# Five norms of a two-block transformer kernel: first block scaled from SBUF, a gate sum and the modulation sums moved, the middle norm's last tile in halves

## The chip, the cores and the metric

The kernel runs on one core of one Trainium2 chip. The metric is the device time of one execution in microseconds (us), as the median of the runs.

## The reference, cut to what matters

Two transformer blocks run over x, 256 tokens of width 1024, in fp32. The norms are what the change is about:

```python
def rmsnorm_2(x, w):
    xf = x.astype(jnp.float32)
    y = xf * lax.rsqrt(jnp.mean(xf * xf, axis=-1, keepdims=True) + EPS)
    return (y * w.astype(jnp.float32)).astype(x.dtype)
...
# first block
u = rmsnorm(h, norm_mix_g[layer])          # norm 0
p = jnp.einsum('bsd,de->bse', u, w_in[layer]) + b_in[layer]
...
u = rmsnorm(h, norm_ffn_g[layer])          # norm 1
z = silu(u @ w_ffn_gate) * (u @ w_ffn_up); h = h + z @ w_ffn_down
return rmsnorm(h, norm_final_g)
# second block
mod = (c_act @ w_ada[l] + b_ada[l])[:, None, :]
sh_m, sc_m, g_m, sh_f, sc_f, g_f = jnp.split(mod, 6, axis=-1)
h = rmsnorm_2(x, norm_mix_w[l]) * (1 + sc_m) + sh_m        # norm 2, on top of norm_final_g's
...
x = x + g_m * (concat(y_ssd, y_att) @ w_out[l])
h = rmsnorm_2(x, norm_ffn_w[l]) * (1 + sc_f) + sh_f        # norm 3
x = x + g_f * conv_ffn(h, w_up[l], ffn_conv_w[l], w_down[l])
return rmsnorm_2(x, final_norm_w)                          # norm 4
```

Norm 2 does two norms in one: the first block's last (with the gain `norm_final_g`) and the second block's first. It therefore needs the sum of squares of the residual and of `Y`, the residual times that gain.

## The kernel before, in words

**The weights** stream from HBM in panels of 4 blocks of 128 rows by 512 columns (1 MB each), two panels ahead, through four slots `raw`. Each product is made of three: ScalarE rounds a panel to `wH` (line 680, 1.9 us), VectorE subtracts to get the rest `wL` (line 1049 by `split_lo`, 2.3 us), and TensorE multiplies high with high, high with low, low with high (lines 1616 and 1619). The normalised activations are split in the same way, into `p1H` and `p1L`. A panel of the "cm" kind is 4 tiles by 4 row blocks by 3 products = 48 products of 256 columns.

**The order of the work** is a list written by hand, `timeline()` (line 119), that every engine walks in order; each engine does its part of each entry and waits on semaphores for the others. So a wait on one engine holds everything behind it there.

**A norm** (lines 748, 1105, 1679, one for each engine) stands between the last panel of one product and the first of the next: norm 0 before `q0`, norm 1 between `out1` and `f0`, norm 2 between `down1` and `xs`, norm 3 between `oo1` and `u0`. Its steps are: VectorE adds the last tile to the residual `res`; ScalarE squares it with a sum (`square`, line 704) and takes the root (`root`, line 726); VectorE inverts it (`turn_over`, line 1087); TensorE spreads the inverse roots over all partitions into `rb`, half of PSUM bank 7 (line 1701); ScalarE copies `rb` to SBUF as `rbs` (line 769). Meanwhile TensorE transposes the residual's 8 column blocks into PSUM (`turn`, line 1556); block 7 lands where block 1 was, so its two transposes are made only after part 0 of the next product (`last_turn`, line 1572). For each block k, VectorE then writes `TMP[k]` = block times gain times `rbs` (line 1137), ScalarE rounds it to `p1H[k]` (lines 781 and 783), VectorE subtracts to `p1L[k]` (`low`, line 1123), and TensorE starts on block k of part 0 of the next product. The loop over k on VectorE is: `TMP[k]`, then `low(k-1)`, then pieces of a weight panel's low half (`first_lo`, `later_lo`). ScalarE has the high halves in the same places, and behind the last `p1H` it goes to the `split_hi` of the next product's next panel, in norm 2 behind one more root, `Ra`, that needs VectorE's sum at line 1151.

**The gates.** In norms 1 and 3, TensorE also sums two gate vectors over the partitions (`gate_sum`, line 1577), the second one ahead of the spread; ScalarE copies out the first, VectorE the second (line 1115).

**The modulation** of the second block is accumulated panel by panel on VectorE and summed over the partitions by TensorE (`ada_sum`, line 1583), 4 products of 64 columns for 512 values, and read by VectorE (`read_ada`, line 1096). Five such sums stand in the feed-forward part (`f3`, `f5`, `f7`, `f9`, `down0`), three inside norm 2 ahead of its spread.

**The last tile in halves.** In norms 1, 3 and 4 the last tile is computed as two halves of 256 columns, the second in bank 6, so that the first can be added and squared while TensorE is on the second (`last_tile`, line 1159). In norm 2 it was one tile of 512 columns.

Of the kernel before, what the change touches and what calls it, by code (L numbers as in the profile page):

```python
# [101 lines left out]
HALF = {1: 1, 3: 2, 4: 3}  # L102
# [16 lines left out]
def timeline():  # L119
# [56 lines left out]
    gemm("down0", [], [("ada_sum", "down0")])  # L176
# [19 lines left out]
def build(nc, IN, out):  # L196
# [17 lines left out]
    with ExitStack() as ctx:  # L214
# [56 lines left out]
        on.in_brow = ctx.enter_context(nc.semaphore("in_brow"))  # L271
        on.half_done = ctx.enter_context(nc.semaphore("half_done"))
# [183 lines left out]
        XA, pre2 = sb("XA", [P, 1]), sb("pre2", [P, 1])  # L456
# [20 lines left out]
        def adaps(where, x):  # L477
            b, c = (x // 2, x % 2 * 4 * NSUM) if where == "norm" else (7, 0)
            return ps[:, b, c:c + 4 * NSUM]

# [9 lines left out]
        HALVES = {"out1": EV["bh1", 2], "oo1": (on.pt_done, 9), "dd1": EV["u9", 2]}  # L490
# [172 lines left out]
        def _(act):  # L663
# [40 lines left out]
            def square(n, i, j):  # L704
# [6 lines left out]
                if n != 2 and 2 * i + j == 3:  # L711
                    act.wait_ge(on.res_half, HALF[n])
                    nc.scalar.activation(sqj[:, 0:T], res[:, 1, W:W + T], ACT.Square, accum_out=XA[:]).then_inc(on.sq_half, 1)
                    cs = slice(W + T, D)
                    if n == 4:
                        store(1, 0)
                act.wait_ge(*EV[f"{RES[n]}{i}", j])
                nc.scalar.activation(sqj[:, cs.start % W:W], res[:, j, cs], ACT.Square,
                                     accum_out=XS[:, i, j:j + 1]).then_inc(on.sq_done, 1)
                if n == 2:  # L720
                    act.wait_ge(on.y_done, 2 * i + j + 1)
                    act.wait_ge(on.sq_done, squares(n, 2 * i + j + 1))
                    nc.scalar.activation(sqj, Y[:, j, half(i)], ACT.Square,
                                         accum_out=YS[:, i, j:j + 1]).then_inc(on.ysq_done, 1)
# [23 lines left out]
            def norm(n):  # L748

                table(ACT.Sqrt)  # L750
                for j in range(TB):
                    if n:
                        square(n, 1, j)
                    else:
                        square_x(j)
                    if n != 2:
                        root(n, j)
                if n == 4:
                    return
                if n == 2:  # L760
                    for j in range(TB):
                        root(n, j)
                if n == 0:
                    first_hi(0, 0, 1)
                if n in GATE_OF:
                    act.wait_ge(on.gate_psum, 2 * GATE_OF[n] + 1)
                    nc.scalar.activation(GATE[GATE_OF[n]][0], ps[:, 2 * GATE_OF[n], :], ACT.Copy).then_inc(on.gate_done, 1)
                act.wait_ge(on.rb_psum, n + 1)
                nc.scalar.activation(rbs, rb, ACT.Copy).then_inc(on.rb_copy, 1)
                for k in range(KD):  # L770
# [4 lines left out]
                    elif n and 0 < k <= KP:  # L775
                        later_hi(n, k - 1)
# [260 lines left out]
        def _(dve):  # L1037
# [48 lines left out]

            def turn_over(n, j):

                if n == 2:
                    dve.wait_ge(on.ysq_done, 3 + j)  # L1090
                    stt(S2[:, j:j + 1], XS[:, 1, j:j + 1], EPS, YS[:, 1, j:j + 1], ALU.mult,
                        ALU.add).then_inc(on.s2_done, 1)
# [12 lines left out]
            def norm(n):  # L1105
                if n in (0, 2):
                    turn_over(n, 0)
                if n == 4:
                    scaled(0, 0)
# [3 lines left out]
                if n in GATE_OF:  # L1113
                    dve.wait_ge(on.gate_psum, 2 * GATE_OF[n] + 2)
                    v.tensor_copy(GATE[GATE_OF[n]][1], ps[:, 2 * GATE_OF[n] + 1, :]).then_inc(on.gate_done, 1)
                if n == 2:
                    read_ada("norm")
                    dve.wait_ge(on.ada_done, 8)
                    stt(am[:], mod[:, 8:16], 1.0, pc("norm_mix_w_2", 0, 8), ALU.add, ALU.mult).then_inc(on.mod_done, 1)
                    stt(af[:], mod[:, 32:40], 1.0, pc("norm_ffn_w_2", 0, 8), ALU.add, ALU.mult).then_inc(on.mod_done, 1)  # L1120
                    dve.wait_ge(on.mod_done, 1)
# [37 lines left out]
            def last_tile(name, n):  # L1159
# [4 lines left out]
                if n == 1:  # L1164
                    tt(left, o[:, 0:T], left, ALU.add).then_inc(on.res_half, 1)
                    step(tt(right, o[:, T:W], right, ALU.add))
                    turn_over(n, 0)
                    dve.wait_ge(on.tile_done, TILE[name, 1])
                    tt(right, o2, right, ALU.add).then_inc(on.evac_dve, 1)
                else:  # L1170
# [7 lines left out]
                    dve.wait_ge(on.res_half, HALF[n])  # L1178
# [3 lines left out]
                dve.wait_ge(on.sq_half, HALF[n])  # L1182
# [754 lines left out]
```

## Time and profile before

| | us |
|---|---|
| runs before: median (lowest to highest) of 3 | 819.65 (819.58 to 819.81) |
| the profiled execution's own time | 819.11 |
| its span, first to last instruction | 817.4 |
| TensorE busy | 796.6 (97%) |
| VectorE busy | 592.8 (73%) |
| ScalarE busy | 495.1 (61%) |

TensorE's granted clock is full in all 40 slices of the page. The profiled execution is 0.54 us below the median, and 1.7 us of it lie outside the span. Busy times of matmuls overlap one another, so the distance from one start to the next is what to read, not the duration in the row.

### The profile page before, as it was taken

The numbers are of one execution on the slowest core, as the hardware profiler recorded it, in microseconds if no ns is written. First come the engines' busy times: TensorE is split into PE (matmuls) and PEld (weight loads), VectorE is DVE, ScalarE is ACT, GpSimd is POOL, SyncE is SP. The second block draws the span as 40 slices with busy tenths as digits, with TensorE's granted clock in tenths as the row PEclk, the third lists the DMA queues.
The fourth block names the chain that finished last, engine by engine and source line by source line (L and its number), as shares of the span: only waits on it lengthen the run. The fifth ranks groups of instructions, "written<-read, shape, count | busy, mean of one in ns | idle before, by whom it ended". The sixth has DMA issues, their size and how long they took to land.

```text
span 817.4 us, 14238 instructions
## 1 busy us (share of the span) xinstructions
PE 796.6 (97%) x5944; PEld 743.7 (91%) x5944; DVE 592.8 (73%) x767; ACT 495.1 (61%) x744; POOL 15.8 (2%) x36
## 2 busy tenths in 40 slices
PE   8999999999999999999999999999999999999996
PEld 8988879999999889999998888899788999999885
DVE  5575685639756868887878886897778977787463
ACT  6777788568836456344444256856756776666452
POOL 3000000000200000000000000000000000000000
PEclk9999999999999999999999999999999999999999
DMA  8873634447553558889898993644351865645611
GB/s 295 287 251 111 206 104 155 155 155 235 164 169 104 171 189 275 274 287 297 263 298 272 342 349 100 235 152 155 102 162 55 275 190 175 199 136 205 229 55 52
DMA packets 105664, 161.15 MB, mean 197 GB/s; under 512 B 4464, under 2 KB 51840, under 8 KB 105600
## 3 DMA queue, kind: packets, MB, share of 16 engines
q1 hardware_dynamic: 105456, 159.97, 59.6%
q8 instruction: 47, 0.77, 0.4%
q10 hardware_dynamic: 144, 0.26, 0.1%
q14 instruction: 17, 0.14, 0.0%
HBM read 159.16 MB, written 1.06 MB: 196 GB/s over the span
## 4 chain that ended last, share of the span: by engine, by line
PE 87%; DVE 7%; ACT 4%; issue 2%; DMA 0%; DVEq 0%; ACTq 0%
PE ps L1616 54%; PE ps L1619 22%; DVE wL L1049 2%; PE ps L1545 2%; ACT wH L680 2%; DVE arena L1049 1%; PE ps L1772 1%; ACT arena L932 1%; DVE arena L1052 1%; PE ps L1590 1%; PE ps L1609 1%; PE ps L1739 1%; PE ps L1819 1%; PE ps L1816 1%; PE ps L1804 0%
## 5 line engine op out<-in xcount | busy, mean ns | idle before, releaser
L1049 DVE TENSOR_TENSOR wL<-raw,wH 128x2048 fp32r<-128x2048 f32 (+2 forms) x133 | 282.9, 2131 | 120.7 <-ACT wH L680 119.5
L1616 PE MATMUL ps<-p1H,wH 128*128 128x256 f32 x1256 | 358.9, 286 | 5.8 <-DVE p1L L1049 1.8
L1616 PE MATMUL ps<-p1L,wH 128*128 128x256 f32 x1256 | 355.3, 283 | 0.0
L1616 PE MATMUL ps<-p1H,wL 128*128 128x256 f32 x1256 | 355.3, 283 | 0.0
L680 ACT ACTIVATE wH<-raw 128x2048 fp32r<-128x2048 f32 (+1 forms) x121 | 225.1, 1867 | 123.7 <-PE ps L1616 65.5
L1616 PEld LDWEIGHTS ps<-p1H,wH 128*128 128x128 f32 x1256 | 240.8, 192 | 9.1 <-issue 6.8
L1616 PEld LDWEIGHTS ps<-p1L,wH 128*128 128x128 f32 x1256 | 240.9, 192 | 0.3 <-issue 0.2
L1616 PEld LDWEIGHTS ps<-p1H,wL 128*128 128x128 f32 x1256 | 240.9, 192 | 0.0
L1619 PE MATMUL ps<-wH,zH 128*128 128x512 f32 x172 | 67.0, 390 | 0.0
L1619 PE MATMUL ps<-wH,zL 128*128 128x512 f32 x172 | 66.9, 389 | 0.0
L1619 PE MATMUL ps<-wL,zH 128*128 128x512 f32 x172 | 66.9, 389 | 0.0
L1052 DVE SCALAR_TENSOR_TENSOR arena<-arena,par 128x256 f32<-128x256 f32 x124 | 50.7, 479 | 9.4 <-ACT arena L864 6.9
L798 ACT ACTIVATE arena<-ps 128x256 f32<-128x256 f32 x86 | 30.1, 378 | 26.2 <-PE ps L1616 25.8
L1052 DVE SCALAR_TENSOR_TENSOR arena<-raw,cact,arena 128x512 f32<-128x512 f32 x56 | 42.0, 751 | 1.7
L1049 DVE TENSOR_TENSOR arena<-arena 128x512 f32<-128x512 f32 (+3 forms) x41 | 35.1, 871 | 6.6 <-ACT arena L819 2.6
L1619 PEld LDWEIGHTS ps<-wH,zH 128*128 128x128 f32 x172 | 32.3, 188 | 6.7
L1619 PEld LDWEIGHTS ps<-wH,zL 128*128 128x128 f32 x172 | 32.3, 188 | 6.7
L1619 PEld LDWEIGHTS ps<-wL,zH 128*128 128x128 f32 x172 | 32.3, 188 | 6.6
L1616 PE MATMUL ps<-pyH,wH 128*128 128x256 f32 x128 | 36.6, 286 | 0.0
L1616 PE MATMUL ps<-pyL,wH 128*128 128x256 f32 x128 | 36.2, 283 | 0.0
L1616 PE MATMUL ps<-pyH,wL 128*128 128x256 f32 x128 | 36.2, 283 | 0.0
L1619 PE MATMUL ps<-wH,p1H 128*128 128x512 f32 (+1 forms) x92 | 34.4, 374 | 0.0
(274 smaller groups left out, 956.9 us busy)
## 6 DMA issues: line engine op xcount, KB each, us to landing
raw<-in_w_in SPq DMA_DIRECT2D x38, 1024.0 KB, 5.2
raw<-in_w_ada SPq DMA_DIRECT2D x24, 1024.0 KB, 5.2
raw<-in_w_up SPq DMA_DIRECT2D x44, 512.0 KB, 4.9
raw<-in_w_ffn_gate SPq DMA_DIRECT2D x22, 512.0 KB, 4.7
raw<-in_w_ffn_up SPq DMA_DIRECT2D x22, 512.0 KB, 6.3
raw<-in_w_ffn_down SPq DMA_DIRECT2D x10, 1024.0 KB, 5.4
raw<-in_w_down SPq DMA_DIRECT2D x10, 1024.0 KB, 5.2
raw<-in_w_out SPq DMA_DIRECT2D x8, 1024.0 KB, 5.0
```

Source lines behind the costliest of these rows:

```text
L680: nc.scalar.activation(wH[:, q % NHL, 0:nk, 0:wd], raw[:, i % NRAW, 0:nk, 0:wd], ACT.Copy).then_inc(on.w_hi, 1)
L798: nc.scalar.activation(dst(m), ps[:, t[1], 0:T], f, **bias).then_inc(on.evac_act, 1)
L932: ins = nc.scalar.activation(p, s if kind == 1 else p, ACT.Exp, scale=scale, bias=NM[:, u % 2, h:h + 1], accum_out=SU[:, u % 2, h:h + 1])
L1049: return v.tensor_tensor(o, a, b, op)
L1052: return v.scalar_tensor_tensor(out=o, in0=a, scalar=s, in1=b, op0=op0, op1=op1)
L1545: return nc.tensor.transpose(o, i, ident[:])
L1590: last = mm(adaps(where, x)[:, t * NSUM:(t + 1) * NSUM], ACC[a + x][:, t * P:(t + 1) * P], ones[:, 0:NSUM], start=True, stop=True)
L1609: last = mm(ps[:, bank, 0:T], at_[:, k0 + k, P:2 * P], wt[:, slot, k, half_of * T:half_of * T + T], start=st and x == 0, stop=k == nk - 1 ...
L1616: last = mm(ps[:, t[1], 0:T], wt[:, slot, k, t[2]:t[2] + P], at_[:, k0 + k, :], start=st, stop=en)
L1619: last = mm(ps[:, t[1], 0:t[3]], at_[:, k0 + k, t[4] * P:(t[4] + 1) * P], wt[:, slot, k, t[2]:t[2] + t[3]], start=st, stop=en)
L1739: last = mm(o, aQ[r, h // 2, n * P:(n + 1) * P], kk[r, ks], start=False, stop=a == nh - 2)
L1772: last = mm(ps[C * x:C * x + C, PVB[u], pair * P:(pair + 1) * P], vv, PT[u][:, slot(nh, hh) * nk + kb, :], start=kb == 0, stop=kb == nk - 1)
```

## The change

1. ScalarE copies transposed block 0 to SBUF (`TMP[:, 0]`), and VectorE scales block 0 from that copy with `rb` in PSUM. The copy of `rb` to `rbs` comes after `p1H[0]` on ScalarE, and `low(0)` comes ahead of `TMP[1]` on VectorE.
2. The transposes of block 6 move from inside the norm to `last_turn`, behind part 0 of the next product.
3. The second gate sum stands behind the spread, in bank 3, and is copied out by ScalarE.
4. The modulation sums: none at `down0` any more, two in norm 2 ahead of the spread, two in norm 2 behind the copy of `rb`; each product has 32 columns instead of 64. `am` is computed at `f9`, `af` behind the last `low` of norm 2. The columns of `w_ada` are loaded in another order.
5. Norm 2's last tile is computed in halves.
6. Norm 0 has four filler products behind its transposes instead of two.

```diff
-ADA_COL = (4, 5, 6, 7, 8, 9, 0, 1, 2, 3, 10, 11)
+ADA_COL = (4, 5, 0, 1, 2, 3, 6, 7, 8, 9, 10, 11)
-SUM_AT = {"f3": (2, 1), "f5": (3, 1), "f7": (4, 1), "f9": (5, 1), "down0": (6, 1), "norm": (7, 3)}
+SUM_AT = {"f3": (2, 1), "f5": (3, 1), "f7": (4, 1), "f9": (5, 1), "norm": (6, 2), "post": (8, 2)}
-NSUM = 64
+NSUM = 32
-HALF = {1: 1, 3: 2, 4: 3}
+HALF = {1: 1, 2: 2, 3: 3, 4: 4}
+PART = {1: 1, 2: 2, 3: 4, 4: 5}
-    gemm("down0", [], [("ada_sum", "down0")])
+    gemm("down0")
-        HALVES = {"out1": EV["bh1", 2], "oo1": (on.pt_done, 9), "dd1": EV["u9", 2]}
+        HALVES = {"out1": EV["bh1", 2], "down1": (on.tmp_done, 16), "oo1": (on.pt_done, 9), "dd1": EV["u9", 2]}
...
 ScalarE, square(n, i, j)
+                    if n == 2:
+                        act.wait_ge(on.res_half, PART[n] + 1)
+                        nc.scalar.activation(sqj[:, T:W], Y[:, 1, W:W + T], ACT.Square, accum_out=YA[:]).then_inc(on.sq_half, 1)
+                        act.wait_ge(on.sq_half, PART[n] + 1)
...
 ScalarE, norm(n)
-                    if n != 2:
-                        root(n, j)
+                    root(n, j)
-                if n == 2:
-                    for j in range(TB):
-                        root(n, j)
+                act.wait_ge(on.ut_psum, 4 * n + 1)
+                nc.scalar.activation(TMP[:, 0], un(0), ACT.Copy).then_inc(on.un0_copy, 1)
                 if n in GATE_OF:
                     act.wait_ge(on.gate_psum, 2 * GATE_OF[n] + 1)
                     nc.scalar.activation(GATE[GATE_OF[n]][0], ps[:, 2 * GATE_OF[n], :], ACT.Copy).then_inc(on.gate_done, 1)
-                act.wait_ge(on.rb_psum, n + 1)
-                nc.scalar.activation(rbs, rb, ACT.Copy).then_inc(on.rb_copy, 1)
                 for k in range(KD):
...
-                    elif n and 0 < k <= KP:
-                        later_hi(n, k - 1)
+                    elif n and 1 < k <= KP + 1:
+                        later_hi(n, k - 2)
...
+                    if k == 0:
+                        act.wait_ge(on.rb_psum, n + 1)
+                        nc.scalar.activation(rbs, rb, ACT.Copy).then_inc(on.rb_copy, 1)
+                    if k == 0 and n in GATE_OF:
+                        act.wait_ge(on.gate_psum, 2 * GATE_OF[n] + 2)
+                        nc.scalar.activation(GATE[GATE_OF[n]][1], ps[:, 3, :], ACT.Copy).then_inc(on.gate_done, 1)
...
 VectorE, norm(n)
-                if n in GATE_OF:
-                    dve.wait_ge(on.gate_psum, 2 * GATE_OF[n] + 2)
-                    v.tensor_copy(GATE[GATE_OF[n]][1], ps[:, 2 * GATE_OF[n] + 1, :]).then_inc(on.gate_done, 1)
...
-                dve.wait_ge(on.rb_copy, n + 1)
                 for k in range(KD):
                     if k in (4, 6, 7):
-                        dve.wait_ge(on.ut_psum, 3 * n + {4: 1, 6: 2, 7: 3}[k])
-                    stt(TMP[:, k], un(k), gain(n, k), rbs, ALU.mult, ALU.mult).then_inc(on.tmp_done, 1)
-                    if k:
+                        dve.wait_ge(on.ut_psum, 4 * n + {4: 2, 6: 3, 7: 4}[k])
+                    if k == 0:
+                        dve.wait_ge(on.un0_copy, n + 1)
+                        dve.wait_ge(on.rb_psum, n + 1)
+                    if k == 1:
+                        low(0)
+                        dve.wait_ge(on.rb_copy, n + 1)
+                    stt(TMP[:, k], un(k) if k else TMP[:, 0], gain(n, k), rbs if k else rb, ALU.mult,
+                        ALU.mult).then_inc(on.tmp_done, 1)
+                    if k > 1:
                         low(k - 1)
...
                 low(KD - 1)
                 if n == 2:
+                    read_ada("post")
+                    dve.wait_ge(on.ada_done, 8)
+                    stt(af[:], mod[:, 32:40], 1.0, pc("norm_ffn_w_2", 0, 8), ALU.add, ALU.mult).then_inc(on.mod_done, 1)
                     dve.wait_ge(on.sq_done, squares(2, 4))
+                    step(tt(XS[:, 1, 1:2], XS[:, 1, 1:2], XA[:], ALU.add))
                     tt(Ra[:], XS[:, 0, :], XS[:, 1, :], ALU.add).then_inc(on.sum_final, 1)
...
 VectorE, last_tile(name, n)
-                if n == 1:
+                if n < 3:
                     tt(left, o[:, 0:T], left, ALU.add).then_inc(on.res_half, 1)
                     step(tt(right, o[:, T:W], right, ALU.add))
+                    if n == 2:
+                        dve.wait_ge(on.res_half, PART[n])
+                        tt(Y[:, 1, W:W + T], left, gfin[:, W:W + T], ALU.mult).then_inc(on.res_half, 1)
+                        sum2(0)
                     turn_over(n, 0)
                     dve.wait_ge(on.tile_done, TILE[name, 1])
                     tt(right, o2, right, ALU.add).then_inc(on.evac_dve, 1)
+                    if n == 2:
+                        dve.wait_ge(*EV[name, 1])
+                        tt(Y[:, 1, W + T:D], right, gfin[:, W + T:D], ALU.mult).then_inc(on.y_done, 1)
...
 TensorE
             def last_turn(n):
+                pe.wait_ge(on.rb_copy, n + 1)
+                turn(n, (6,), range(TB)).then_inc(on.ut_psum, 1)
                 pe.wait_ge(on.tmp_done, 8 * n + 2)
                 turn(n, (7,), range(TB)).then_inc(on.ut_psum, 1)
...
-                mm(ps[:, 2 * g + i, :], ones[:], ACC[10 * g + i], start=True, stop=True).then_inc(on.gate_psum, 1)
+                mm(ps[:, 3 if i else 2 * g, :], ones[:], ACC[10 * g + i], start=True, stop=True).then_inc(on.gate_psum, 1)
...
-                    if n in GATE_OF:
-                        gate_sum(GATE_OF[n], 1)
+                    last.then_inc(on.ut_psum, 1)
                     if n == 2:
                         ada_sum("norm")
...
                     last.then_inc(on.rb_psum, 1)
+                    if n in GATE_OF:
+                        gate_sum(GATE_OF[n], 1)
                     stream_in(n, 1, 1)
                     turn(n, (4, 5), range(TB)).then_inc(on.ut_psum, 1)
-                    pe.wait_ge(on.rb_copy, n + 1)
-                    turn(n, (6,), range(TB)).then_inc(on.ut_psum, 1)
+                    if n == 2:
+                        pe.wait_ge(on.rb_copy, n + 1)
+                        ada_sum("post")
                     if n == 0:
-                        warm(2)
+                        warm(4)
```

## Rows read from the trace of the kernel before

**Rows 1.** The page, busy time, share and instructions of each engine.

```profile
PE 796.6 (97%) x5944; PEld 743.7 (91%) x5944; DVE 592.8 (73%) x767; ACT 495.1 (61%) x744; POOL 15.8 (2%) x36
```

**Rows 2.** Waits of TensorE: waited for, us in total, times, longest.

```profile
PE ps L1616 <- DVE wL L1049: 0.8, 1, 0.8
```

**Rows 3.** Timeline, TensorE in norm 1: start, us, instruction, idle before.

```profile
296.66 1.04 PE L1545 MATMUL ps<-ident,res 128*128 128x128 f32 x8
297.53 1.02 PE L1581 MATMUL ps<-acc,ones 128*128 128x512 f32 x2
298.39 0.61 PE L1549 MATMUL ps<-ident,R 128*128 128x128 f32 x4
...
301.11 0.35 PE L1616 MATMUL ps<-p1H,wH 128*128 128x256 f32 x1 [1.19 <-DVE p1L L1049]
...
306.93 0.38 PE L1545 MATMUL ps<-ident,res 128*128 128x128 f32 x2
```

**Rows 4.** Timeline, ScalarE in norm 1.

```profile
295.08 0.42 ACT L713 ACTIVATE arena<-res 128x256 f32<-128x256 f32 x1
...
299.04 0.38 ACT L769 ACTIVATE arena<-ps 128x256 f32<-128x256 f32 x1 [1.21 <-PE ps L1549]
...
306.16 1.28 ACT L670 ACT_TABLE_LOAD   x1
...
307.87 0.42 ACT L781 ACTIVATE p1H<-arena 128x256 fp32r<-128x256 f32 x1 [0.21 <-DVE arena L1052]
```

**Rows 5.** Timeline, VectorE in norm 1 and at panel f0.

```profile
299.46 0.88 DVE L1052 SCALAR_TENSOR_TENSOR arena<-ps,par,arena 128x256 f32<-128x256 f32 x2 [0.17 <-ACT arena L769]
...
307.35 0.48 DVE L1052 SCALAR_TENSOR_TENSOR arena<-ps,par,arena 128x256 f32<-128x256 f32 x1 [1.33 <-PE ps L1545]
...
310.13 2.29 DVE L1049 TENSOR_TENSOR wL<-raw,wH 128x2048 fp32r<-128x2048 f32 x1 [0.49 <-ACT wH L680]
```

**Rows 6.** Timeline, VectorE in norm 0 and at panel q0.

```profile
9.45 0.51 DVE L1049 TENSOR_TENSOR p1L<-arena,p1H 128x256 fp32r<-128x256 f32 x1
...
15.82 0.48 DVE L1052 SCALAR_TENSOR_TENSOR arena<-ps,par,arena 128x256 f32<-128x256 f32 x1
...
20.45 2.29 DVE L1049 TENSOR_TENSOR wL<-raw,wH 128x2048 fp32r<-128x2048 f32 x1 [1.38 <-ACT wH L680]
```

**Rows 7.** Timeline, TensorE behind part 0 of q0.

```profile
15.86 0.38 PE L1545 MATMUL ps<-ident,res 128*128 128x128 f32 x2
```

**Rows 8.** Timeline, TensorE in norm 2 and behind product bc.

```profile
498.80 0.36 PE L1616 MATMUL ps<-p1H,wH 128*128 128x256 f32 x1 [1.27 <-issue]
...
525.90 1.06 PE L1545 MATMUL ps<-ident,arena 128*128 128x128 f32 x8 [0.49 <-DVE ADT L1049]
```

**Rows 9.** Timeline, ScalarE in norm 2.

```profile
493.45 0.63 ACT L718 ACTIVATE arena<-res 128x512 f32<-128x512 f32 x1 [1.18 <-DVE res L1049]
...
495.52 0.29 ACT L738 ACTIVATE R<-S,pre 128x1 f32<-128x1 f32 x1 [0.34 <-DVE S L1052]
496.66 0.38 ACT L769 ACTIVATE arena<-ps 128x256 f32<-128x256 f32 x1 [0.85 <-PE ps L1549]
```

**Rows 10.** Timeline, VectorE behind part 0 of xs.

```profile
505.05 0.48 DVE L1052 SCALAR_TENSOR_TENSOR arena<-ps,am,arena 128x256 f32<-128x256 f32 x1 [0.74 <-PE ps L1545]
...
509.70 2.29 DVE L1049 TENSOR_TENSOR wL<-raw,wH 128x2048 fp32r<-128x2048 f32 x1 [2.15 <-ACT wH L680]
```

**Rows 11.** Chain that ended last: start, us, what.

```profile
440.00 0.84 PE ps L1590 x8
...
535.25 1.46 PE ps L1866 x14
```

**Rows 12.** Timeline, TensorE's first product behind norm 3.

```profile
623.29 0.35 PE L1616 MATMUL ps<-p1H,wH 128*128 128x256 f32 x1 [1.37 <-DVE p1L L1052]
```

**Rows 13.** Timeline, VectorE in norm 3 and at panel u0.

```profile
620.27 0.16 DVE L1094 RECIPROCAL R<-R 128x1 f32<-128x1 f32 x1 [0.88 <-ACT R L738]
...
632.39 4.49 DVE L1049 TENSOR_TENSOR wL<-raw,wH 128x2048 fp32r<-128x2048 f32 x2 [0.44 <-ACT wH L680]
```

More of the change, by code:

```diff
@@ L477, in adaps @@
         def adaps(where, x):
-            b, c = (x // 2, x % 2 * 4 * NSUM) if where == "norm" else (7, 0)
+            b, c = (0, x * 4 * NSUM) if where == "norm" else (7, T + x * 4 * NSUM if where == "post" else 0)
             return ps[:, b, c:c + 4 * NSUM]
@@ L710, in square @@
                 cs = half(i)
-                if n != 2 and 2 * i + j == 3:
-                    act.wait_ge(on.res_half, HALF[n])
+                if 2 * i + j == 3:
+                    act.wait_ge(on.res_half, PART[n])
                     nc.scalar.activation(sqj[:, 0:T], res[:, 1, W:W + T], ACT.Square, accum_out=XA[:]).then_inc(on.sq_half, 1)
+                    if n == 2:
+                        act.wait_ge(on.res_half, PART[n] + 1)
+                        nc.scalar.activation(sqj[:, T:W], Y[:, 1, W:W + T], ACT.Square, accum_out=YA[:]).then_inc(on.sq_half, 1)
+                        act.wait_ge(on.sq_half, PART[n] + 1)
                     cs = slice(W + T, D)
@@ L716, in square @@
                         store(1, 0)
+                junk = sqj[:, cs.start % W:W]
                 act.wait_ge(*EV[f"{RES[n]}{i}", j])
-                nc.scalar.activation(sqj[:, cs.start % W:W], res[:, j, cs], ACT.Square,
-                                     accum_out=XS[:, i, j:j + 1]).then_inc(on.sq_done, 1)
+                nc.scalar.activation(junk, res[:, j, cs], ACT.Square, accum_out=XS[:, i, j:j + 1]).then_inc(on.sq_done, 1)
                 if n == 2:
@@ L722, in square @@
                     act.wait_ge(on.sq_done, squares(n, 2 * i + j + 1))
-                    nc.scalar.activation(sqj, Y[:, j, half(i)], ACT.Square,
-                                         accum_out=YS[:, i, j:j + 1]).then_inc(on.ysq_done, 1)
+                    nc.scalar.activation(junk, Y[:, j, cs], ACT.Square, accum_out=YS[:, i, j:j + 1]).then_inc(on.ysq_done, 1)
             def root(n, j):
@@ L1085, in before, with sum2 @@
                     v.tensor_scalar(pre[:], XS[:, 0, :], 1.0 / D, EPS, ALU.mult, ALU.add).then_inc(on.pre_done, 1)
+            def sum2(j):
+                dve.wait_ge(on.ysq_done, 3 + j)
+                stt(S2[:, j:j + 1], XS[:, 1, j:j + 1], EPS, YS[:, 1, j:j + 1], ALU.mult, ALU.add).then_inc(on.s2_done, 1)
             def turn_over(n, j):
[L1089 to L1092, printed above, removed]
                 dve.wait_ge(on.rt_done, 2 * n + j + 1)
@@ L1105, in norm @@
             def norm(n):
-                if n in (0, 2):
+                if n == 0:
                     turn_over(n, 0)
+                if n == 2:
+                    sum2(1)
                 if n == 4:
@@ L1181, in last_tile @@
                     tt(right, gt[:, 0:T], right, ALU.add).then_inc(on.evac_dve, 1)
-                dve.wait_ge(on.sq_half, HALF[n])
-                stt(pre2[:], XA[:], 1.0 / D, pre[:, 1:2], ALU.mult, ALU.add).then_inc(on.pre2_done, 1)
+                dve.wait_ge(on.sq_half, PART[n] + (n == 2))
+                if n == 2:
+                    step(stt(pre2[:], XA[:], EPS, YA[:], ALU.mult, ALU.add))
+                    stt(pre2[:], pre2[:], 1.0 / D, pre[:, 1:2], ALU.mult, ALU.add).then_inc(on.pre2_done, 1)
+                else:
+                    stt(pre2[:], XA[:], 1.0 / D, pre[:, 1:2], ALU.mult, ALU.add).then_inc(on.pre2_done, 1)
                 if n == 4:
@@ L1344, in _ @@
                     read_ada(e[1])
+                    if e[1] == "f9":
+                        dve.wait_ge(on.ada_done, 4)
+                        stt(am[:], mod[:, 8:16], 1.0, pc("norm_mix_w_2", 0, 8), ALU.add, ALU.mult).then_inc(on.mod_done, 1)
                 elif k == "scores":
@@ L1652, in panel @@
                                 pe.wait_ge(*BANKFREE[name, m])
+                            if k == 0 and m == 3 and name in ("f0", "u0"):
+                                pe.wait_ge(on.gate_done, 2 if name == "f0" else 4)
                             last = product(t, k)
@@ L1685, in _ @@
                         stream_in(0, 0, j)
-                        turn(0, range(4), (j,))
+                        last = turn(0, range(4), (j,))
                     if n in GATE_OF:
@@ L1691, in _ @@
                         stream_in(n, 0, 1)
-                        turn(n, range(4), range(TB))
-                    if n in GATE_OF:
-                        gate_sum(GATE_OF[n], 1)
+                        last = turn(n, range(4), range(TB))
+                    last.then_inc(on.ut_psum, 1)
                     if n == 2:
@@ L1831, in _ @@
                     pe.wait_ge(on.u_ready, 24)
+                    pe.wait_ge(on.ada_done, 8)
                     for kk in range(KD):
```

12 lines of the change are left out of this document (5 added, 7 removed).

## The prediction

> **What bounds the kernel now.** I read the page first. TensorE is busy for 796.6 of 817.4 us and VectorE for 73% [rows 1], with the clock full throughout, so a change can gain only the few places where TensorE waits, and can lose wherever it makes a new one. Then I read the waits of TensorE and the timelines of all three engines around the norms. The reader is to see two chains in each norm. The **front chain** is last root, spread, copy of `rb`, `TMP[0]`, `p1H[0]`, `low(0)`, first product: TensorE stands idle at its end, 1.19 us in norm 1 [rows 3], 1.27 in norm 2 [rows 8], 1.37 in norm 3 [rows 12]. The **back chain** starts behind part 0 of the next product: last transposes, `TMP[7]`, `p1H[7]`, then the split of the next product's panel on ScalarE and VectorE. It is nearly late already: behind norm 0 TensorE waits 0.8 us for it [rows 2], and behind norm 1 `wL` is ready at 310.13 + 2.29 = 312.42 [rows 5], while TensorE comes there at 306.93 + 0.14 (two transposes) + 5.8 (48 products at 0.12) = 312.87 [rows 3], 0.45 later. The change works on the front chain and lengthens the back one.
>
> **Norm 1.** Front: the gate sum leaves the path (297.53 to 298.39 [rows 3]) and so does the copy of `rb` (299.04 to `TMP[0]` at 299.46, 0.42 [rows 4, 5]). The spread then starts at about 297.55 and `TMP[0]` at 298.2 instead of 299.46. The new copy of block 0 (0.38, as the copy of `rb` [rows 4]) runs on ScalarE beside the spread, since the transposes end at 297.53; the gate copies stand behind `p1H[0]` or before it is due. `TMP[1]` behind `low(0)` delays block 1 to about 300.9, and it is due at 301.3. So the first product comes 1.2 earlier, at 299.9, and part 0 ends 1.2 earlier, at 305.7.
> Back: the transposes of block 6 are now made only there. Four transposes instead of two cost TensorE 0.22 more (eight take 0.87 [rows 3]). What counts is the order behind them. VectorE reaches `TMP` 0.42 behind the transposes (306.93 to 307.35 [rows 3, 5]): before, that was block 7, now it is block 6, with `low(5)` and block 7 another 0.8 behind (two operations issued 0.4 apart). On ScalarE the table load, 306.16 before and so hidden in the wait for block 7 [rows 4], now stands behind the late `p1H[6]`: 305.7 + 0.42 = 306.15 `TMP[6]`, 306.67 `p1H[6]`, 307.1 table load, 308.5 `p1H[7]` (1.4 behind the load: itself and its small operation), against 307.87 [rows 4]. From `p1H[7]` to the start of `wL` take the 2.26 of before (307.87 to 310.13 [rows 4, 5]): 310.75, ready 313.05. TensorE would come at 305.7 + 0.36 + 5.8 = 311.9 and waits 1.15. Against 312.87 the norm costs **+0.2**. The whole front gain goes into that wait.
>
> **Norm 3.** The gate sum saves nothing: the last inverse root runs from 620.27 to 620.43 [rows 13], when the sum is just done. Left is the copy, 0.42: first product 622.87 instead of 623.29 [rows 12]. Back: there is no table load, but `TMP[7]` is 0.8 later behind part 0, net 0.4 later; `wL` starts 632.76 instead of 632.39 [rows 13] and is ready at 635.05, which is when TensorE came before. **+0.05**.
>
> **Norm 0.** The first product is bound by `low(0)` at 9.45 [rows 6], which does not move. `TMP[1]`, which was made in the wait ahead of it, comes behind it: 0.4 more on VectorE, 0.2 of it reaching block 1. Part 0 ends at 16.06 instead of 15.86 [rows 7]. `TMP[6]` started at 15.82 [rows 6] and now starts at 16.06 + 0.42 = 16.48, 0.66 later, and with it the rest down to `wL` at 20.45 [rows 6], for which TensorE waited already [rows 2]. **+0.66**. The two more filler products run in idle time; the first product comes 0.6 behind their end.
>
> **Norm 2.** The last tile in halves costs TensorE 0.15, hidden by the front chain. For the root, two squares of 512 columns, from 493.45, ended in the root at 495.52 [rows 9]. Now the first root waits for the left half of `Y`, at about 492.8, and four quarter squares follow, 0.42 [rows 4] plus a read, some 0.52 apart, with two waits of 0.1: 493.0 + 2.1 + 0.1 + 0.3 is again 495.5. Bounds: 0.5 earlier, if nothing waits for the first root, to 0.3 later; I take 0. The copy of `rb` leaves the path (0.42 and a little): `TMP[0]` at 496.66 [rows 9] and the first product could start at 498.3 instead of 498.80 [rows 8]. But TensorE's queue now holds, ahead of it, two modulation sums that wait for that copy, and ScalarE makes the copy behind `p1H[0]`: 497.6 to 498.0. A sum takes 0.84 for 8 passes [rows 11], 0.88 with its edges, so the product starts at 498.0 + 1.76 = 499.8, **1.0 later**. Back: `TMP[7]` comes 1.0 + 0.8 later than 505.05 [rows 10]. Behind the last `low` VectorE has four more small operations, two reads, `af` and a sum with its wait, 0.55 together, and ScalarE's root `Ra` and the split stand behind them: `wL` starts 2.35 later than 509.70 [rows 10], at 512.05, and is ready at 514.35, just when TensorE has done its own 1.2 later work (514.5). That is not the end of it. VectorE and ScalarE are a closed chain from there to `ADT`, and TensorE waited 0.49 for that at 525.90 [rows 8]. So product q2 starts the full **+2.35** later.
>
> **The sum at down0** is gone: **-0.88** [rows 11]. The four others of the feed-forward part stay. Narrower products save nothing: passes of 8 columns take 1.46 for 14 [rows 11], 0.104 each, and those of 64 columns 0.84 for 8, 0.105. The order of the columns of `w_ada` moves no byte more or less, and no queue issues another transfer; SyncE's wait for the last `low` of norm 2 passes some 1.8 later, less than TensorE's own delay. `am` at `f9` is 0.1 on an idle engine.
>
> **Sum:** 0.66 + 0.2 + 2.35 + 0.05 - 0.88 = **+2.4 us**. The profiled execution took 819.11, 0.54 below the median; it would take 821.5, and the median 819.65 becomes **822.0**. 0.2%, about what can be told from no change, is 1.6 us: the limits are 818.0 and 821.3.
>
> **Rivals.**
> *A, the back chain does not end anything.* If ScalarE came to each split early enough, 4.2 before TensorE is due, only fronts and transposes would count: norm 0 +0.4, norm 1 -1.0, norm 3 -0.2, norm 2 +1.2, down0 -0.88, together -0.5: **819.2**, not slower. For it: latencies of 0.1 to 0.3 that I carried over may vanish. Against it: the margin before was 0.45 in norm 1 and negative in norm 0, and the transposes of block 6 are moved by the code itself. Chance 0.12.
> *B, narrow products are cheap.* If 32 columns cost half of 64, the four sums at f3 to f9 and the two behind the spread save 0.42 each, 2.5 together: **819.5**. The 8-column rows speak against it. Chance 0.06. The Trainium skill, TensorE: Matmul & The Clock Gate, in its section Step-by-step: what each phase is for, says throughput is purely as many cycles as columns; by that B would hold, and here the trace disagrees.
> *C, it is worse.* The weight transfers behind norm 2 issue late, because SyncE waits for the slots that VectorE frees 2.35 later, and collide: 1 us more, **823.0**. Chance 0.07.
> *D, mixed.* Parts of A in one or two norms, or the roots of norm 2 0.5 earlier: 819.5 to 820.9. Chance 0.15.
> My forecast has 0.60, with 820.9 to 823.0 as its own range.
>
> **Numbers.** The range 819.3 to 823.0 takes in the forecast, D, B and part of A. Slower by over 0.2%: most of the forecast and C, 0.60. Within 0.2%: B, D, A's middle and the forecast's low end, 0.33. Faster: A and B together, or a margin I misread in norm 2, 0.07.
>
> **What would show it.** Right: first product behind norm 1 about 1.2 earlier in the norm, and a new wait of about 1 us for `wL` at f1; in norm 2, 16 passes of sums between the copy of `rb` and the first product, and a wait for `ADT` of 1.5 to 2 instead of 0.49; behind norm 0, 1.4 instead of 0.8 for `wL`. Wrong: no wait for `wL` at f1, passes of the sums under 0.08 apart, or the last root of norm 2 over 0.3 earlier behind the end of down1.

## The result, and the profile of the changed kernel

The changed kernel takes **825.84 us** as the median of four executions (824.78 to 826.78), against 819.73 for the kernel before in the same comparison: a ratio of 1.0073, 95% interval 1.0055 to 1.009. The sign was forecast; the size was not. 822.0 was predicted, and 823.0 was the upper end of the range. The profiled execution took 824.78 with a span of 823.1, so it lies 5.67 above that of the kernel before. It is the fastest of the four; two took 826.6 and 826.8, so the median lies 6.1 above.

The page of the changed kernel, TensorE's busy time and the granted clock in the 40 slices:

```profile
PE 801.0 (97%) x5960; PEld 748.3 (91%) x5960; DVE 592.9 (72%) x771; ACT 497.5 (60%) x754; POOL 16.1 (2%) x36
PEclk9999999999999999999999999999999999999998
```

The page looks like that of the kernel before [rows 1]. Its slices are 20 us wide and a slice of 90% or more shows as 9, so 3 us at a lower clock would not be seen here. Five of TensorE's waits in the changed kernel (us in total, times, longest); two larger entries, 4.4 in seven waits for `arena` and 2.2 at the start, are the same in both kernels:

```profile
PE ps L1572 <- DVE ADT L1056: 1.5, 1, 1.5
PE ps L1645 <- DVE p1L L1056: 1.5, 3, 0.6
PE ps L1645 <- ACT arena L805: 1.4, 2, 0.9
PE ps L1619 <- ACT arena L788: 1.0, 1, 1.0
PE ps L1645 <- DVE wL L1056: 0.9, 1, 0.9
```

Two of these waits were forecast: 1.5 instead of 0.49 for `ADT` (a tensor that VectorE makes and TensorE transposes behind product bc), and 0.9 at f1. That one is put down to ScalarE's copying out of f0's results, with `wL` ready at the same moment, at 314.14. For `wL` in norm 0 1.4 was forecast, and it is 0.9 instead of 0.8. None of them is 3 us long. Where the rest went is seen in the timeline of TensorE in the changed kernel (start, us, instruction, idle before):

```profile
16.45 0.60 PE L1572 MATMUL ps<-ident,res 128*128 128x128 f32 x4
23.85 0.38 PE L1645 MATMUL ps<-p1H,wH 128*128 128x256 f32 x1 [0.89 <-DVE wL L1056]
297.77 1.03 PE L1572 MATMUL ps<-ident,res 128*128 128x128 f32 x8
301.02 0.35 PE L1645 MATMUL ps<-p1H,wH 128*128 128x256 f32 x1 [0.47 <-DVE p1L L1056]
306.84 0.60 PE L1572 MATMUL ps<-ident,res 128*128 128x128 f32 x4
314.20 0.38 PE L1645 MATMUL ps<-p1H,wH 128*128 128x256 f32 x1 [0.89 <-ACT arena L805]
493.93 1.87 PE L1619 MATMUL ps<-ones,arena 128*128 128x32 f32 x16
498.20 1.97 PE L1619 MATMUL ps<-ones,arena 128*128 128x32 f32 x16 [1.03 <-ACT arena L788]
500.01 0.36 PE L1645 MATMUL ps<-p1H,wH 128*128 128x256 f32 x1
...
502.10 0.41 PE L1645 MATMUL ps<-p1H,wH 128*128 128x256 f32 x1
...
503.38 0.41 PE L1645 MATMUL ps<-p1H,wH 128*128 128x256 f32 x1
...
507.33 0.60 PE L1572 MATMUL ps<-ident,arena 128*128 128x128 f32 x4
...
529.93 1.06 PE L1572 MATMUL ps<-ident,arena 128*128 128x128 f32 x8 [1.52 <-DVE ADT L1056]
628.40 0.35 PE L1645 MATMUL ps<-p1H,wH 128*128 128x256 f32 x1 [0.62 <-ACT brow L791]
815.85 0.28 PE L1638 MATMUL ps<-wL,zH 128*128 128x256 f32 x1
```

Five rows of TensorE in the kernel before, which these are measured against:

```profile
6.53 0.60 PE L1545 MATMUL ps<-ident,res 128*128 128x128 f32 x4
...
22.80 0.39 PE L1616 MATMUL ps<-p1H,wH 128*128 128x256 f32 x1 [0.82 <-DVE wL L1049]
...
493.33 2.79 PE L1590 MATMUL ps<-ones,arena 128*128 128x64 f32 x24
...
504.63 0.38 PE L1545 MATMUL ps<-ident,arena 128*128 128x128 f32 x2
...
810.18 0.28 PE L1609 MATMUL ps<-wL,zH 128*128 128x256 f32 x1
```

From 502.10 to 503.38 lie six products, 0.213 each; before, 48 such products and the step to the transposes took 5.82, 0.12 each (301.11 to 306.93 [rows 3]). The granted clock explains it. The changed kernel by stretches (PE, PEld, DVE, ACT and POOL busy, then PEclk, DMA share, GB/s):

```profile
496.00:500.00 4.00, 2.83 (x23) 2.49 (x23) 2.68 (x9) 2.22 (x6) 0.00 (x0) 1.00 0.00 0
500.00:504.00 4.00, 4.00 (x23) 4.00 (x23) 3.63 (x7) 3.01 (x7) 0.00 (x0) 0.59 0.01 4
528.00:531.00 3.00, 1.48 (x12) 1.06 (x10) 0.35 (x2) 2.99 (x3) 0.00 (x0) 1.00 0.90 279
531.00:535.00 4.00, 3.49 (x17) 3.52 (x18) 3.80 (x4) 3.97 (x10) 0.00 (x0) 0.57 0.24 62
```

and the kernel before in the same places:

```profile
500.00:504.00 4.00, 4.00 (x35) 4.00 (x35) 3.88 (x9) 2.42 (x7) 0.00 (x0) 1.00 0.01 4
528.00:532.00 4.00, 4.00 (x36) 4.00 (x35) 4.00 (x7) 3.97 (x6) 0.00 (x0) 1.00 0.30 68
```

Twice, for some 3.4 us each (0.41 of 4 us is missing, at a level of 0.5), TensorE is granted 1.2 GHz instead of 2.4: right behind the thin stretch of norm 2, and right behind the wait for `ADT`. It is counted as fully busy there, with 23 products in 4 us instead of 35. Part 0 of xs takes 7.32 (500.01 to the transposes at 507.33) instead of 5.83 (498.80 [rows 8] to 504.63), so one such stretch costs **1.5**.

With that the time can be laid out by checkpoints. The second column is how much later the changed kernel comes there, the third what was added since the row above, and the fourth how much of that is the lower clock, at 1.5 for each stretch:

| checkpoint | changed | step | of it lower clock | forecast of the step |
|---|---|---|---|---|
| product q1 behind norm 0 (23.85) | +1.05 | +1.05 | | +0.66 |
| transposes of norm 1 (297.77) | +1.11 | +0.06 | | 0 |
| first sum of norm 2 (493.93) | +0.60 | -0.51 | | +0.2 - 0.88 = -0.68 |
| transposes behind `ADT` (529.93) | +4.03 | +3.43 | 1.5 | +2.35 |
| first product behind norm 3 (628.40) | +5.11 | +1.08 | 1.5 | -0.42 |
| last product of dd (815.85) | +5.67 | +0.56 | | +0.47 |

Without the two stretches 2.7 remain, where 2.4 was forecast.

### The profile page after: what moved, and what is told of

Same layout as the page of the kernel before. It is cut to its first block and busy times, and to the rows that moved or that the text cites. A ratio compares the mean times of both kernels' runs of the same rounds, so it can differ in the third digit from the quotient of the medians.

```text
span 823.1 us, 14290 instructions
## 1 busy us (share of the span) xinstructions
PE 801.0 (97%) x5960; PEld 748.3 (91%) x5960; DVE 592.9 (72%) x771; ACT 497.5 (60%) x754; POOL 16.1 (2%) x36
## 3 DMA queue, kind: packets, MB, share of 16 engines
HBM read 159.16 MB, written 1.06 MB: 195 GB/s over the span
```

## The experiments

Twelve kernels ran. The theory behind most of them, **K**: the schedule costs what was forecast, and the rest is a lower granted clock that comes where TensorE stands empty or does thin work. The rival, **L**: the lower clock has another cause, or the schedule itself costs more. Ratios are to the kernel before, measured beside each. The mean clock of an execution is on record for all of them, the place of a stretch only for the one that was profiled.

**Fillers in norm 2** (`warm(4)`: four products of 128 columns on the identity, two passes each, computing nothing that is used), ahead of the wait for the copy of `rb`, where TensorE stood idle for 1.03:

```diff
                     turn(n, (4, 5), range(TB)).then_inc(on.ut_psum, 1)
                     if n == 2:
+                        warm(4)
                         pe.wait_ge(on.rb_copy, n + 1)
```

> The changed kernel with four 128-column filler products in norm 2, between the transposes of blocks 4 and 5 and the wait for the copy of rb, where TensorE stood empty for 1.03 us. In the changed kernel's trace the granted clock is at its lower level (1.2 GHz) for 3.4 us from 500.7 and again for 3.4 us from 531.3. Theory K (the clock): the first stretch follows from that empty stretch with the thin work around it, and costs 1.7 us; with the fillers it is gone, the time is 824.1, the second stretch stays. Rival S (the schedule): the extra time is waits, the clock follows by chance or from the sums' narrow products themselves; the fillers change nothing, 825.8, and the stretch from 500.7 stays.

Measured: 821.72 (821.38 to 823.99), ratio 1.0025 (1.0016 to 1.0034). Rows of this kernel:

```profile
496.63 1.06 PE L1581 MATMUL ps<-ident 128*128 128x128 f32 x8
497.82 1.97 PE L1619 MATMUL ps<-ones,arena 128*128 128x32 f32 x16
...
528.07 1.06 PE L1572 MATMUL ps<-ident,arena 128*128 128x128 f32 x8 [1.51 <-DVE ADT L1056]
...
812.52 0.28 PE L1638 MATMUL ps<-wL,zH 128*128 128x256 f32 x1
```

```profile
500.00:504.00 4.00, 4.00 (x35) 4.00 (x35) 3.29 (x6) 2.64 (x6) 0.00 (x0) 1.00 0.02 4
530.00:534.00 4.00, 4.00 (x36) 4.00 (x35) 4.00 (x7) 3.97 (x7) 0.00 (x0) 1.00 0.24 55
```

Eight passes in a time that was idle anyway make the kernel 4.1 faster than the changed one by the medians, and 3.3 by the profiled executions (821.47 to 824.78). The schedule is the same: from the first sum of norm 2 (493.55 here) to the late sums it is 4.27 in both. From that sum to the transposes behind `ADT` it takes 34.52 instead of 36.00. Both stretches are gone, the second too, against the expectation, though the wait of 1.51 for `ADT` is still there. Why the second went with the first, 30 us behind the fillers, is not shown. The last product comes 2.34 later than before (812.52 to 810.18); the forecast was +2.4.

**Fillers there and ahead of the wait for `ADT`** (six more, in bank 5).

> As the run before, and six more fillers at the transposes behind product bc, where TensorE waited 1.5 us for ADT. Theory K: both stretches at the lower clock are gone, 822.4, which is the time that the prediction gave; its sum of waits was then right and only the clock was left out. Rival S: 825.8. If the second stretch has another cause (the first one's delay), 824.1 and one stretch left.

Measured: 821.64 (821.45 to 822.73), 1.0025 (1.0015 to 1.0035). With the lower clock gone already, more fillers gain nothing.

**The sums as before the change** (64 columns, one at down0, three in norm 2, both factors behind them; everything else changed):

```diff
-SUM_AT = {..., "norm": (6, 2), "post": (8, 2)}
-NSUM = 32
+SUM_AT = {..., "down0": (6, 1), "norm": (7, 3)}
+NSUM = 64
```

> The changed kernel with part 4 undone: one sum at down0 again, three in norm 2 ahead of the spread, none behind it, 64 columns, columns of w_ada in the old order, am and af in norm 2. Theory K: no empty stretch before sums, no lower clock in norm 2; product xs starts 1.5 earlier, q2 2.05 earlier, down0 0.88 later: 825.8 - 3.4 - 2.05 + 0.88 = 821.2, ratio to the kernel before 1.002. Rival S without the clock as a term: 825.8 - 1.2 = 824.6.

Measured: 821.34 (821.06 to 823.39), 1.0025 (1.0016 to 1.0035). Its profiled execution, at 823.39 one of the slower ones:

```profile
500.00:504.00 4.00, 3.54 (x29) 3.57 (x30) 3.73 (x9) 3.33 (x9) 0.00 (x0) 1.00 0.02 4
530.00:534.00 4.00, 3.87 (x20) 3.90 (x21) 4.00 (x5) 3.97 (x8) 0.00 (x0) 0.58 0.19 28
```

Only the second stretch is left, here behind a wait of 1.16 for `ADT`. So it does not need the first. Norm 2 itself holds 24 passes of 64 columns and 1.35 of idle here, and the clock stays up. Of the ten executions three have a mean clock of 0.995 and take 823.0 to 823.4; of the seven at 0.997 or 0.998 six take 821.1 to 821.4. By these clocks the same program gets the stretch in one execution and not in the next.

**Block 6's transposes back in the norm** (in norm 2 behind the two late sums; norm 0 has three filler products instead of four):

```diff
                     turn(n, (4, 5), range(TB)).then_inc(on.ut_psum, 1)
+                    if n == 0:
+                        warm(3)
+                    pe.wait_ge(on.rb_copy, n + 1)
                     if n == 2:
-                        pe.wait_ge(on.rb_copy, n + 1)
                         ada_sum("post")
-                    if n == 0:
-                        warm(4)
+                    turn(n, (6,), range(TB)).then_inc(on.ut_psum, 1)
...
-                pe.wait_ge(on.rb_copy, n + 1)
-                turn(n, (6,), range(TB)).then_inc(on.ut_psum, 1)
                 pe.wait_ge(on.tmp_done, 8 * n + 2)
```

> The changed kernel with part 2 undone: the transposes of block 6 stand in the norm again, behind the copy of rb (in norm 2 behind the two sums as well), so that TMP[6] does not wait for part 0. If the back chain ends what the prediction said: 0.4 gained in norm 0, 0.9 in norm 1 (no wait for wL at f1), 0.4 in norm 3, 0.8 in norm 2 and up to q2, 2.5 together: 823.3, with both stretches at the lower clock still there. If the back chain does not end it, only 0.22 for each of the four norms: 825.0.

Measured: 820.93 (820.11 to 822.35), 1.0017 (1.0007 to 1.0026), 2.4 below what was expected. Five executions lie at 820.1 to 820.4 with a mean clock of 0.996, five at 821.4 to 822.4 with 0.994. The profiled one, of the first kind:

```profile
498.00:502.00 4.00, 4.00 (x23) 4.00 (x23) 3.88 (x8) 3.10 (x7) 0.00 (x0) 0.57 0.02 4
...
530.00:534.00 4.00, 4.00 (x36) 4.00 (x35) 4.00 (x8) 3.98 (x6) 0.00 (x0) 1.00 0.43 119
```

Only the first stretch stands in this trace. The mean clocks fit one stretch in the five faster executions and two in the five slower ones. The wait for `ADT` is down to 1.0. The median of the five slower ones, 822.1, is still 1.2 below what was expected with both stretches; the expectation started from the changed kernel's median, and half of its executions had a lower clock still.

**The same with fillers** (`warm(4)` ahead of the wait in norm 2).

> The kernel with block 6's transposes back in the norm, plus four filler products in norm 2 ahead of the wait for the copy of rb, where TensorE stands idle anyway. The kernel without the fillers took 820.93 with one stretch of lower clock in its faster runs and two in its slower ones, each worth 1.7. Theory K (idle and thin work there bring the lower clock): the stretches go, 818.6 or so, faster than the kernel before. Theory L (the lower clock has another cause): no change from 820.9.

Measured: 818.95 (818.26 to 819.95), 0.9986 (0.9977 to 0.9994), and no stretch of lower clock in its trace before the tail of the kernel. For the stretch in norm 2, K is confirmed a second time.

**Block 6 and the sums both as before**; kept are the copy of block 0, the order of `low(0)`, the late gate sum and the last tile in halves. Norm 0 has three filler products here too.

> The changed kernel with parts 2 and 4 undone: block 6's transposes stand in the norm again, and the sums stand as before the change (64 columns, one at down0, three in norm 2 with both factors behind them). Kept are the copy of block 0, the order of low(0), the second gate sum behind the spread, and the last tile of norm 2 in halves. Schedule theory S (the terms of the prediction hold, and a lower granted clock comes only where TensorE stood nearly empty in norm 2): norm 0 +0.4, norm 1 -1.0, norm 3 -0.2, norm 2 -0.4, so about 818.5, with no stretch of clock at the lower level before the end. Theory K2 (the lower clock comes with the earlier copy of block 0 itself): one such stretch of 3.4 us at the norm or at the wait for ADT, 820.2.

Measured: **818.04** (817.7 to 818.69), 0.9979 (0.997 to 0.9987). This version beats both kernels. Rows of its TensorE, and one of its waits:

```profile
6.99 1.06 PE L1570 MATMUL ps<-ident,res 128*128 128x128 f32 x4
7.84 0.92 PE L1579 MATMUL ps<-ident 128*128 128x128 f32 x4
...
493.40 2.79 PE L1615 MATMUL ps<-ones,arena 128*128 128x64 f32 x24
...
525.77 1.06 PE L1570 MATMUL ps<-ident,arena 128*128 128x128 f32 x8 [0.68 <-DVE ADT L1056]
...
622.76 0.36 PE L1641 MATMUL ps<-p1H,wH 128*128 128x256 f32 x1
```

```profile
PE ps L1641 <- DVE wL L1056: 0.8, 1, 0.8
```

Norm 1 starts at 297.79 here, 1.13 later than before. Most of that comes from norm 0, where four passes take 0.85 (6.99 to 7.84), while before four took 0.44 from 6.53 on; the input itself was there no later (first transposes at 4.37 and 4.42). That is the ratio of the two clock levels, but the windows view gives a granted clock of 1.00 there, so the reason is not shown. Such a slow start differs from one execution to the next. The sums of norm 2 start at 493.40, 0.07 later than before: 1.06 is gained from norm 1 to there. The transposes behind `ADT` come 0.13 earlier, so norm 2 gains 0.20, and the first product behind norm 3 0.53 earlier, which is 0.40 more. These are rival A's terms for norms 1 and 3, about -1.0 and -0.2.

From the executions without lower clock the two withdrawn parts get their prices: block 6 behind the product costs 821.72 - 818.95 = **2.8** (and 821.3 - 818.0 = 3.3 with the old sums), the reordered sums 818.95 - 818.04 = **0.9**. The two kernels of each block 6 pair ran in different comparisons, in which the kernel before took 819.81 and 820.06, so these two prices could be 0.25 larger.

**Norm 0 as before as well** (`rb` copied first, `low(0)` behind `TMP[1]`).

> The kernel with parts 2 and 4 undone, and norm 0 entirely as before the change as well (rb copied first, TMP[0] and TMP[1] from it, low(0) behind them). Theory S: norm 0 gives back its 0.4 to 0.6, so 0.5 below that kernel, about 818.0. Rival: nothing on norm 0's first product or on its wait for wL hangs on the order of these operations, and it takes the same time.

Measured: 818.19 (817.66 to 819.19), 0.9979 (0.9971 to 0.9988): the same time, not 0.5 less. The rival holds, as far as eleven executions of each can tell. The order of these operations in norm 0 is worth nothing that shows.

**Only narrower products, in the kernel before.**

```diff
-NSUM = 64
+NSUM = 32
```

> The kernel before with modulation products of 32 columns instead of 64 and nothing else. Theory S (a pass costs the same at 8, 32 and 64 columns): no difference, 819.7. Rival B (half the columns, half the time): eight sums on the path save 0.42 each, some 3 us, 816.6.

Measured: 819.84 (819.09 to 822.02), 1.0006 (0.9998 to 1.0015). The three sums of norm 2:

```profile
493.31 2.76 PE L1590 MATMUL ps<-ones,arena 128*128 128x32 f32 x24
```

24 passes take 2.76, against 2.79 with 64 columns (493.33 above). Rival B is refuted. But five of its twelve executions take 821.7 to 822.0 at a mean clock of 0.996, where the other seven take 819.1 to 819.9 at 0.998 or 0.999 and none of the 35 executions of the kernel before is under 0.997. So halving the columns seems to bring a stretch of lower clock in some executions. The profiled one had none, so its place isn't shown.

The last four ask what TensorE has to do for the clock to fall. Three of them are the kernel before with one thing added in norm 2.

**Idle only**: the product waits for `low(2)` instead of `low(0)`.

```diff
                     turn(n, (6,), range(TB)).then_inc(on.ut_psum, 1)
+                    if n == 2:
+                        pe.wait_ge(on.u_ready, 19)
```

> The kernel before, in which the first product of xs in norm 2 waits for low(2) instead of low(0). Nothing is computed differently; TensorE only stands idle for some 2.7 us there instead of 1.27. The product comes 1.4 later, and the chain behind it too: without a lower clock 821.1. Theory I (an empty TensorE is enough to bring the lower clock): a stretch of 3.4 us at 1.2 GHz behind it, 1.7 more, 822.8. Theory N (it takes the narrow passes): 821.1, and no such stretch.

Measured: 823.49 (822.35 to 825.33), 1.0043 (1.0031 to 1.0055).

The first product of xs, and the stretch behind it:

```profile
501.63 0.39 PE L1616 MATMUL ps<-p1H,wH 128*128 128x256 f32 x1 [3.06 <-DVE p1L L1052]
```

```profile
502.00:506.00 4.00, 4.00 (x25) 4.00 (x24) 3.28 (x6) 1.91 (x4) 0.00 (x0) 0.62 0.02 4
```

An empty engine, with nothing added to the passes that were there before, is enough: theory I. The Trainium skill, TensorE: Matmul & The Clock Gate, section HAM oscillation: how this bites in real kernels, says that a TensorE left waiting is put back to its lower clock, so that what follows starts slow; the trace agrees that the lower level follows a wait, here of 3.06. But the first ten products behind the wait still ran 0.12 apart (501.63 to 502.80), and only then came the slow ones. In the changed kernel no single wait of TensorE from norm 2 to `ADT` was over 1.52.

**Thin and full passes**: 16 matmuls of 32 columns behind block 6's transposes, and the same with 128. Each stands in the trace as two passes, 32 in all, which I had not counted in: they take 3.5 instead of 1.8 and delay the product by 2.2 instead of 0.6.

```diff
+                    if n == 2:
+                        for _ in range(16):
+                            mm(ps[:, 3, 0:32], ident[:], ident[:, 0:32], start=True, stop=True)
```

> The kernel before with 16 extra passes of 32 columns in norm 2 behind block 6's transposes, in a bank that is free. They fill the 1.27 us in which TensorE stood idle and run on for some 0.6: without a lower clock 820.3. Theory N (narrow passes bring the lower clock): in all or some executions a stretch at 1.2 GHz behind them, 822.0. Theory I (it takes an empty engine): 820.3 in all.

> As the kernel with 16 extra narrow passes, but each of 128 columns. The prediction's rows give a pass about the same time at either width, so the schedule is the same. Theory N and theory I both expect no lower clock here and 820.3; if it is as slow as its narrow twin, the width has nothing to do with it. The pair tells apart what the extra work costs and what its narrowness costs.

Measured: thin 823.19 (822.03 to 823.59), 1.0036 (1.0024 to 1.0048); full 821.65 (821.33 to 823.54), 1.0022 (1.0013 to 1.0032). Thin, then full:

```profile
498.30 3.66 PE L1709 MATMUL ps<-ident 128*128 128x32 f32 x32
```

```profile
502.00:506.00 4.00, 4.00 (x22) 4.00 (x22) 3.19 (x6) 1.81 (x4) 0.00 (x0) 0.59 0.00 0
```

```profile
499.78 3.74 PE L1709 MATMUL ps<-ident 128*128 128x128 f32 x32
```

```profile
502.00:506.00 4.00, 4.00 (x37) 4.00 (x36) 3.88 (x9) 2.78 (x7) 0.00 (x0) 1.00 0.02 4
```

The schedule is the same: from the first of the 32 passes to the first product it is 3.49 in both, 0.11 for a pass, and TensorE counts as busy throughout. The thin twin falls to 1.2 GHz behind the passes. From the first sum of norm 2 to the transposes behind `ADT` it takes 36.13 (494.26 to 530.39) and the full one 34.63 (495.74 to 530.37), 1.50 less, and by the medians it is 1.5 slower. The intervals of the two ratios overlap, so it is the traces, one of each, that carry this. That of the full twin is of its slowest execution, at 823.54: its norm 2 began 2.4 later than in the kernel before, with the clock up, and its other eight executions took 821.3 to 821.8. Three of the five executions of the thin one have a clock of 0.996 or 0.997 and take 823.2 to 823.6, two have 0.998 and take 822.0 and 822.6. So neither theory alone: an empty engine brings the lower clock, and one kept busy with narrow passes does too.

**The changed kernel with 64 columns** in all sums but the two behind the spread.

> The changed kernel with 64 columns instead of 32 in all sums but the two behind the spread: the four of the feed-forward part and the two ahead of the spread. A pass costs the same, so without a lower clock it is 821.7, and the schedule is that of the changed kernel. Theory N: wider passes ahead of norm 2's waits keep the clock up in part or in full, 821.7 to 823.5. Theory I: 825.8 as the changed kernel.

Measured: 826.45 (821.39 to 826.81), 1.0063 (1.0044 to 1.0083). Its profiled execution, at a mean clock of 0.991:

```profile
498.00:502.00 4.00, 3.63 (x20) 3.63 (x21) 3.65 (x9) 3.32 (x9) 0.00 (x0) 0.63 0.00 0
502.00:506.00 4.00, 4.00 (x21) 4.00 (x21) 1.88 (x3) 1.18 (x3) 0.00 (x0) 0.51 0.01 4
532.00:536.00 4.00, 3.48 (x20) 3.27 (x19) 3.04 (x3) 3.97 (x10) 0.00 (x0) 0.65 0.30 116
```

Here the lower level lasts some 6.8 us, twice as long as in the changed kernel, and begins within the late sums; behind the wait for `ADT` (1.51) it comes again. Wider columns ahead of the wait do not help, while fillers in the wait did. One of its six executions took 821.39 at a clock of 0.997, where the profiled one has 0.991: the same program, by its clock with none of the stretches, is 5 us faster.

## Why the prediction was wrong, point by point

- **The step that failed** is the premise in the first paragraph, "with the clock full throughout", which was carried over to the changed kernel. Every term was a time at 2.4 GHz. The change leaves TensorE in norm 2, between 495.6 and 500.0, with eight spread and transpose passes, 1.03 of idle and 16 passes of 32 columns. The clock fell behind that, and again behind the wait for `ADT`: 3.0 of the 5.67. The profiled execution has a mean clock of 0.993, as has one other; the two slowest of the four (826.6 and 826.8) have 0.991. The kernel with 64 columns has that clock too where it was traced, with the stretch of norm 2 at double length; that this is so in the two slowest executions here as well is likely, and not shown. For the stretch in norm 2 the fillers (821.72, 818.95) show the cause in two kernels, and the thin and full twins show it in the kernel before. For the stretch behind `ADT` the cause stays open: it came behind waits of 1.52 and 1.16, stayed away behind one of 1.51, and comes in some executions of a program only.
- **Norm 1** went as forecast. The first product comes 3.25 behind the transposes instead of 4.45 [rows 3], 1.2 earlier, and a wait of 0.89 at f1 takes it back. Net with the sum at down0 -0.51, forecast -0.68; with block 6 in the norm and the sum still at down0, 1.06 is gained.
- **Norm 2** had the order that was forecast: 16 passes between the copy of `rb` and the product, and 1.52 for `ADT`. Its +3.43 is 1.5 of clock and 1.93 of schedule, forecast 2.35; with the fillers it is 1.95. The term that was too large is "1.0 later" for the first product: from the first sum of the norm to it are 6.08 (493.93 to 500.01) instead of 5.47, which is 0.6.
- **Norm 3** +0.17 (-0.39 ahead of the product and +0.56 behind it), forecast +0.05.
- **Norm 0** came out at +1.05, forecast +0.66. With the fillers in norm 2, which come later, it is 23.49 - 22.80 = +0.69, so the forecast was right there. The other 0.36 is a weight transfer: in the changed kernel's trace ScalarE waits for a block of `w_in`,

```profile
9.89 0.63 ACT L687 ACTIVATE wH<-raw 128x512 fp32r<-128x512 f32 x1 [0.19 <-DMA raw<-in_w_in]
```

  and starts that rounding 0.35 later than in the kernel with the fillers (9.54, no wait); VectorE, and block 1's first product (12.03 to 11.67), follow by as much.
- **The sum of the schedule, +2.4, held**: 821.72 against 819.81 with the fillers is +1.9, and +2.34 by the last product in the traces. That it fits so closely is partly luck: 0.4 too much in norm 2 is made up by 0.2 too little up to there and 0.1 in norm 3.
- **Rivals.** B is refuted by the row of 24 passes. A is refuted by the waits, yet names what the front chain would be worth without block 6's move. C is not seen: from 505 to 560, behind norm 2, no engine waits for a weight transfer. D asked for parts of A or for earlier roots in norm 2, and without the lower clock the time is 821.7, above its range. No rival held the clock, and none was slow enough. The whole range lacked it.

What the trace of before could have told: its norm 2 already had 1.27 of idle [rows 8] behind six transposes and 24 passes of 64 columns, and the change put more thin passes and a later product there. It could not tell the price, since its clock never fell there. With the price measured since, a rival "the clock falls once" would have stood at 822.0 + 1.5 = 823.5, and one "twice" at 825.0.

## What to carry to other kernels

When an edit adds idle or narrow passes to a stretch where TensorE is already thin, give the clock a rival of its own, priced by the products behind it: here 1.5 us per stretch, more than any schedule term but norm 2's. Look at the granted clock by stretches of 1 to 4 us, since a page in 40 slices hides it and TensorE still counts as fully busy. Moving work from the front of a stage to its back pays only where the back has a margin: with 0.45 of margin, two transposes moved behind the product in each of four norms cost some 3 us together, while the copy, the order, the late gate sum and the last tile in halves without that move gained 2.0 (818.04 against 820.06).

## What was not expected of the hardware

- The lower clock is not tied to a wait of one length. It came behind 3.06 of idle, behind 3.66 of narrow passes without idle, and in the changed kernel behind 1.03 of idle with narrow passes around it. It did not come behind 3.74 of passes of 128 columns, nor behind 1.27 and 1.35 of idle after passes of 64 columns, nor in the profiled execution with the wait of 1.51 for `ADT` and fillers earlier on.
- It differs between executions of one program by whole steps: 820.1 to 820.4 and 821.4 to 822.4 for one kernel, 821.39 and 826.8 for another.
- A pass of an fp32 matmul costs TensorE 0.10 to 0.11 at 8 and 64 columns [rows 11], and at 32 and 128 (3.49 for 32 passes of either width). The narrow one saves no time and can cost some, by the clock behind it.
